# Two attention blocks with heads in halves of TensorE's rows and columns, rotation by a lane shuffle, compression in column halves

## What is computed

```python
def apply_rope(x, cos, sin):                       # on each head of 64
    x1, x2 = jnp.split(x, 2, axis=-1)
    return jnp.concatenate([x1 * c - x2 * s, x2 * c + x1 * s], axis=-1)

# layer 0, nsa_mixer: 16 query heads in 4 groups, three kinds of keys (kc, ks, kw) and values
q, kc, vc, ks, vs, kw, vw, gt = jnp.split(h @ w_in, splits, axis=-1)
def compress(t, pe, w1, w2):                       # 15 blocks of 32 tokens, every 16
    blk = (t[:, :, cidx] + pe).reshape(b, g, n_cmp, CMP_LEN * hd)
    return jax.nn.gelu(blk @ w1) @ w2
s_cmp = einsum('bgrqd,bgcd->bgrqc', q, kc) * scale # and its softmax p_cmp
o_slc = ...  # keys of chosen blocks of 64; with 256 tokens all 4 blocks are chosen: causal softmax
o_win = ...  # window of 512 over 256 tokens: causal softmax too
o = gates[0] * o_cmp + gates[1] * o_slc + gates[2] * o_win

# layer 1, swa_mixer: 16 query heads, 2 key heads, window 128, a sink for each head
p = exp(s - m); p = p / (sum(p) + exp(sink - m))
```

## Time and profile before

| | us |
|---|---|
| median of 3 runs | 1258.78 (1254.45 to 1262.51) |
| the profiled execution, whole | 1250.05 |
| its span | 1248.3 |
| PE busy in it | 1184.7 (95%) |
| DVE, ACT, POOL busy | 754.8, 564.7, 453.4 |

### The profile page before, as it was taken

The page is one execution under the profiler, slowest core; times in us unless marked ns, Lnnn a source line. Parts: engine busy times, 40 slices in busy tenths (PEclk is TensorE's granted clock), DMA queues, the critical chain, the costliest instruction groups (busy, mean ns, idle before and its releaser), DMA issues.

```text
span 1248.3 us, 23831 instructions
## 1 busy us (share of the span) xinstructions
PE 1184.7 (95%) x9314; PEld 1123.8 (90%) x9314; DVE 754.8 (60%) x1076; ACT 564.7 (45%) x789; POOL 453.4 (36%) x427
## 2 busy tenths in 40 slices
PE   7898999999999888999999999998989898999998
PEld 7896779999999865999999998997988897999998
DVE  5834664767645657676765565447664757767643
ACT  4232444545444344455454436645344544545432
POOL 5622331366620443166660211113430403666500
PEclk9997999999999989999999999999999999999999
DMA  8551102667655440466665464233432452767552
GB/s 261 174 181 34 35 1 66 203 173 196 174 182 176 146 136 1 125 179 180 190 180 180 154 193 133 76 102 102 135 102 69 135 167 72 196 174 194 176 185 85
DMA packets 226409, 175.50 MB, mean 141 GB/s; under 512 B 8720, under 2 KB 207632, under 8 KB 226208
## 3 DMA queue, kind: packets, MB, share of 16 engines
q1 hardware_dynamic: 220896, 168.89, 45.3%
q10 hardware_dynamic: 5408, 5.55, 1.4%
q0 software_dynamic: 32, 0.03, 0.0%
HBM read 173.40 MB, written 1.05 MB: 140 GB/s over the span
## 4 chain that ended last, share of the span: by engine, by line
PE 82%; DVE 8%; ACT 3%; issue 3%; POOL 3%; DMA 0%; DVEq 0%; SPq 0%; ACTq 0%; POOLq 0%
PE bank L587 22%; PE bank L593 22%; PE bank L588 22%; PE bank L862 2%; DVE w_l L1581 2%; PE bank L621 2%; ACT w_h L1204 2%; PE bank L726 1%; PE bank L1064 1%; PE bank L830 1%; PE bank L627 1%; POOL work L2346 1%; DVE work L1697 1%; PE bank L870 1%; PE bank L714 1%
## 5 line engine op out<-in xcount | busy, mean ns | idle before, releaser
L587 PE MATMUL bank<-xh,w_h 128*128 128x256 f32 (+2 forms) x1792 | 450.4, 288 | 8.4 <-ACT w_h L1256 7.0
L588 PE MATMUL bank<-xl,w_h 128*128 128x256 f32 (+2 forms) x1792 | 442.8, 284 | 0.0
L587 PEld LDWEIGHTS bank<-xh,w_h 128*128 128x128 f32 x1792 | 339.3, 189 | 11.0 <-ACT w_h L1256 7.0
L588 PEld LDWEIGHTS bank<-xl,w_h 128*128 128x128 f32 x1792 | 340.2, 190 | 0.9
L1581 DVE TENSOR_TENSOR w_l<-raw,w_h 128x2048 fp32r<-128x2048 f32 x94 | 210.3, 2237 | 160.8 <-ACT w_h L1204 160.5
L1204 ACT ACTIVATE w_h<-raw 128x2048 fp32r<-128x2048 f32 x94 | 171.4, 1823 | 229.4 <-PE bank L593 215.7
L593 PE MATMUL bank<-xh,w_l 128*128 128x256 f32 (+2 forms) x1792 | 251.4, 283 | 2.9 <-DVE w_l L1581 2.9
L593 PEld LDWEIGHTS bank<-xh,w_l 128*128 128x128 f32 x1792 | 230.5, 189 | 3.3 <-DVE w_l L1581 3.1
L2268 POOL TENSOR_TENSOR work<-work 128x256 f32<-128x256 f32 x66 | 163.0, 2470 | 139.8 <-ACT work L1351 139.8
L1865 DVE TENSOR_TENSOR w_l<-raw,w_h 128x2048 fp32r<-128x2048 f32 x66 | 151.3, 2293 | 14.0 <-ACT w_h L1347 14.0
L587 PE MATMUL bank<-hid_h,w_h 128*128 128x256 f32 (+1 forms) x592 | 147.0, 283 | 2.5 <-issue 1.8
(11 more groups left out here) (299 smaller groups left out, 1578.0 us busy)
## 6 DMA issues: line engine op xcount, KB each, us to landing
raw<-in_ffn_w_gu SPq DMA_DIRECT2D x88, 512.0 KB, 4.9
raw<-in_w_in SPq DMA_DIRECT2D x26, 1024.0 KB, 5.3
raw<-in_ffn_w_down SPq DMA_DIRECT2D x40, 512.0 KB, 4.5
raw<-in_w_ffn_up SPq DMA_DIRECT2D x22, 512.0 KB, 4.0
raw<-in_w_ffn_gate SPq DMA_DIRECT2D x22, 512.0 KB, 5.2
raw<-in_w_ffn_down SPq DMA_DIRECT2D x20, 512.0 KB, 4.6
raw<-in_nsa_w_in SPq DMA_DIRECT2D x9, 1024.0 KB, 5.5
raw<-in_swa_w_qkv SPq DMA_DIRECT2D x5, 1024.0 KB, 5.3
```

Source lines behind the costliest of these rows:

```text
L587: mm(dst, parts[0][:, k, cols], high, start=first, stop=False)
L588: mm(dst, parts[0][:, k, cols], low, start=False, stop=False)
```

## The change

- **Rotation.** Within each head the features are stored in an order in which the partner of a feature stands 16 lanes away inside the same 32 (the weights are permuted on the host, and the sine carries the sign). `permute` is gone from PE; DVE makes the partner by a `stream_shuffle` into `xr` and then multiplies by the sine.
- **Order of layer 0.** Chunks kc, vc, the eight of the queries, gates, then the keys and values. The gathering into blocks moves from DVE (16 instructions) to ACT (32 copies, before `high(4)`), without the position term, which enters as a 61st column. All loads of w1 are issued by SP, two behind slab 2 and two behind slab 4. `compress` runs twice, after chunks 7 and 11, with the blocks (61 columns) as weights and w1 (256 columns) streaming, keys into PSUM rows 0 to 60 and values into 64 to 124, one after the other in turn; then a copy, two transposes, four gelus. The scores of the compressed keys, their softmax and the first scores of pair 0 run between the last chunks; `keep_busy` before the attention is gone.
- **Attention of layer 0.** Keys keep both heads' halves in one tile without zeros; score matmuls contract over 64 rows, alternating between rows 0 to 63 (head 0, one PSUM bank) and 64 to 127 (head 1, another bank). Value products alternate between the column halves. Second and third unit get their scores together. One of three copies out of PSUM goes to ACT; the splits of slabs 11 and 12 are cut into pieces of 512 columns, one in each round. Four buffers instead of three.
- **Attention of layer 1.** One unit for each pair (both heads, both halves of the queries), 8 in all; scores of pairs 0 and 1 already run behind chunks 6 and 8 of the projections.
- Two remaining fillers are 11 and 19 matmuls of 384 columns instead of 8 and 14 of 512.

```diff
-        NSA = [(8, 1), (9, 1), (10, 0), (11, 0), ("k", 0), ("k", 2), (12, 0), (13, 0), ("k", 4), ("k", 6), (14, 0), (15, 0),
-               (16, 0)] + [(i, 1) for i in range(8)]
+        NSA = [(8, 1), (9, 1), (10, 0), (11, 0)] + [(i, 1) for i in range(8)] + [(16, 0), ("k", 0), ("k", 2), ("k", 4), ("k", 6),
+               (12, 0), (13, 0), (14, 0), (15, 0)]
...
-                mm(bank[4 + k % 2][:, 0:T1], E("rot"), xs[:, k % 2, :], start=True, stop=True).then_inc(perm_done, 1)
...
+                line.put(V.stream_shuffle(xr[:, k % 2, :], xs[:, k % 4, :], [j ^ 16 for j in range(32)]))
+                line.settle()
...
+                line.put(V.tensor_tensor(tsin[:, k % 2, :], xr[:, k % 2, :], E("sin"), ALU.mult), sin_done)
...
                 for p in range(8 * half, 8 * half + 8):
-                    for hc in range(2):
+                    for kv in range(2):
-                        last = mm(bank[7 - kv][:, 60 * hc:60 * hc + 60], w1[:, p % 8, 128 * hc:128 * hc + 128],
-                                  blkT[:, kv, p, :], start=p == 0 and hc == 0, stop=p == 15, skip_group_check=True)
+                        last = mm(bank[7][64 * kv:64 * kv + 61, 0:256], blkT[:, kv, p, :], cmp_w[half][:, kv, p % 8, :],
+                                  start=p == 0, stop=p == 15, skip_group_check=True)
...
+                for b in range(2):
+                    for a in range(2):
+                        last = mm(bank[4 + a][:, 128 * b:128 * b + 128], q_half(ci, a, 0), k_half(4 * b + ci // 2, a, 128),
+                                  start=False, stop=True, skip_group_check=True)
...
+                for b in range(2):
+                    for kb in range(2):
+                        for a in range(2):
+                            at = 256 * b + 128 * kb
+                            last = value_piece(O, a, 1, S_pt[:, (p + a) % 4, at:at + 128], b, kb, g)
...
+            for i in range(1, 8 + 2):
+                if i <= 8:
+                    part_turn(3 * i - 3)
+                if i < 8:
+                    first_scores(i)
+                if i >= 2:
+                    second_values(i - 2)
+                if i <= 8:
+                    part_turn(3 * i - 2)
+                if i < 8:
+                    second_scores(i)
+                if i <= 8:
+                    first_values(i - 1)
+                    part_turn(3 * i - 1)
...
+                for i in range(2, 8 + 2):
+                    pair_turn(i - 2)
+                    if i < 8:
+                        pair_scores(i)
+                    pair_values(i - 2)
```

More of the change, by code:

```diff
@@ L610, in chunk @@
                 line["n"] += 1
-            def keep_busy(b, n):
-                for _ in range(n):
-                    mm(bank[b][:, 0:512], ident_b[:, :], mask_b[:, 0:256].unsqueeze(1).broadcast_to([128, 2, 256]), start=True,
-                       stop=True, skip_group_check=True)
             def turn(ins, signal):
@@ new lines, in _ @@
+                if n == 18:
+                    cmp_turn()
+                    pe.wait_ge(cmp_kv_taken, 6)
+                    pe.wait_ge(vt_taken, 1)
+                    first_scores(0)
+                if n >= 19:
+                    w = n - 19
+                    if w:
+                        second_scores(0)
+                    pe.wait_ge(proj_taken, 19 + 2 * w)
+                    turn([(bank[2 + w][:, 256 * kb + 128 * j:256 * kb + 128 * j + 128],
+                              big1[:, 12 + 2 * w + j, 128 * kb:128 * kb + 128]) for kb in range(2) for j in range(2)], vt_done)
@@ new lines, in _ @@
+            high(2)
+            high(3)
+            act.wait_ge(meta_ss, 1)
+            line.put(fn(meta_rstd[:, :], bank[6][:, 0:META], ACT.Sqrt, bias=eps_col[:, 0:1]), meta_root)
+            act.wait_ge(proj_taken, 4)
+            blocks(1)
+            act.wait_ge(roped, 2)
+            blocks(0)
+            high(4)
+            high(5)
+            high(6)
+            high(7)
+            act.wait_ge(cmp_hid, 2)
+            act.wait_ge(prepared, 4)
+            for kv in range(2):
+                at = slice(64 * kv, 64 * kv + 61)
+                line.put(fn(hid_sb[at, :], bank[7][at, 0:256], ACT.Copy), cmp_raw)
@@ new lines, in _ @@
+            high(8)
+            act.wait_ge(vt_done, 1)
+            line.put(fn(egate.rearrange("p a b -> p (a b)"), bank[5][:, 0:96], ACT.Exp, scale=-1.0), vt_taken)
+            act.wait_ge(cmp_hidt, 1)
+            hid = bank[6][:, 0:256].rearrange("p (h k c) -> p h k c", h=2, k=2)
+            line.put(fn(pe_b, hid[:, :, :, 60], ACT.Copy))
+            line.settle()
+            for kv in range(2):
+                for hc in range(2):
+                    line.put(fn(hidT[:, kv, hc, :], hid[:, hc, kv, 0:60], ACT.Gelu_apprx_tanh, bias=pe_b[:, hc, kv:kv + 1]), cmp_act)
@@ L1333, in _ @@
-            attention(NSA_UNITS, 0, True, 0)
+                line.put(fn(vc_rep[32 * r:32 * r + NCMP, :], bank[4][0:NCMP, 0:256], ACT.Copy), cmp_kv_taken)
+            fn(scrap, eps_col[:, 0:1], ACT.Exp)
+            high(10)
+            act.wait_ge(cmp_centered, 1)
+            line.put(fn(c_e, c_s, ACT.Exp, scale=SCALE), cmp_exp)
+            for qb in range(2):
+                act.wait_ge(cmp_turned, qb + 1)
+                line.put(fn(c_pt[:, qb, :, :].rearrange("p a b -> p (a b)"), bank[6 + qb][:, :], ACT.Copy), cmp_pt)
@@ L1447, in _ @@
                              vt_taken)
-            attention(SWA_UNITS, V_SWA, False, 8)
+                if n == 8:
+                    pair_exp(0)
+            pair_exp(1)
+            for i in range(2, 8 + 3):
+                if i >= 3:
+                    attention_high(i - 3, False)
+                if i < 10:
+                    ci = i - 2
+                    act.wait_ge(at_turned, V_SWA + 2 * ci + 2)
+                    if ci >= 2:
+                        act.wait_ge(at_pv, 16 + ci - 1)
+                    line.put(fn(S_pt[:, 2 * (ci % 2) + 1, 0:384], bank[3][:, 0:384], ACT.Copy), at_pt_act)
+                if i < 8:
+                    pair_exp(i)
             squares(3, T1, xT, taken(N_SWA_O), lambda c: high(M_SWA + 7 + c // 2) if c % 2 else None)
@@ L2232, in ropes @@
                     else:
+                        if table is NSA:
+                            pool.wait_ge(cmp_hid, 2)
                         for g in range(2):
```

776 lines of the change are left out of this document (414 added, 362 removed).

## The result

| | before | changed |
|---|---|---|
| median, first measurement | 1256.62 us (1253.60 to 1262.51, 4 runs) | 1222.49 us (1212.78 to 1227.75, 4 runs) |
| the same, measured again | 1252.57 us (1244.88 to 1262.57, 11 runs) | 1223.74 us (1215.69 to 1227.43, 6 runs) |
| profiled execution, whole | 1250.05 | 1217.23 |
| its span | 1248.3 | 1215.4 |

The changed kernel is faster: its time over that of the kernel before, the ratio, is 0.9732 with a 95% interval of 0.9684 to 0.9780, and 0.9764 (0.9720 to 0.9809) when measured again. The prediction was 1207 us with a range of 1190 to 1228. In the profiled executions 32.8 us are saved; the forecast was 51.7.

A forecast was written before the change was run, and what follows sets the result against it. PE was taken to bound layer 0's attention, PE and the chain together layer 1. Savings of 41.4 us (layer 0) and 10.3 (layer 1), 51.7 of 1250.05, gave 1198.4 profiled, scaled to a median of 1207 us, range 1190 to 1228.

The forecast's parts named there:

- PE's list in the projections of layer 0: Layer 0 from 17.8 us: chunks 54.0, compression 6.9, moved-in work 10.2 and small items, in all 74.7 us of PE work.
- Its waits: PE's expected waits in the projections of layer 0: sum 11.8 us, less 1 that overlaps, 10.8.
- 74.7 + 10.8: Layer 0 projections: PE's work plus waits, added to the 17.8 us start, put the attention rounds' start at 103.3 us.
- Compression: Layer 0: 64 passes of 0.217 us, 13.9 serially, 6.9 with column halves overlapping; ACT copies together 8 us.
- A round: Layer 0's attention: PE work 6.3 us, no gain taken for first scores; 6.6 us taken per round.
- the chain: Layer 0's attention, round to round: transposes, first scores, maximum, ACT, evacuation and wait, gates, POOL, hand-overs; given as 6.6 us.
- Layer 1: Attention start about 9.5 us behind the last chunk, 3.85 us a pair, end at 485.4 us instead of 495.7: 10.3 less.
- rival 3: DVE and ACT become the bound: a round of 8.2 us, projections lose 10 more, 1228 us in all; 14%.
- 1: Array halves don't overlap when changing at every matmul: round 9.3 us on PE, compression 13.9, 1237 us in all; 5%.
- 2: Each change of half drains the array, 0.14 us a change, 38 us on top of non-overlapping halves: 1275 us; 3%.
- 4: Gaps in the new rounds keep PE's clock low: round 11.0 us, layer 1 pair 5.3, 1251 us in all; 4%.
- 5: More gain than forecast: no waits in the projections and rounds of 5.9 us, 1190 us in all; 4%.

The follow-up runs named there:

- the kernel with all orders: Changed kernel with layer 1's start reordered, layer 0's waits removed, maximum ahead of factor, and three more edits of order; 1201.58 us, ratio 0.9594.

## Why the prediction was right, and where it was off

The median of 1222.5 us lies inside the range and 15.5 above the forecast. In the profiled execution 18.9 us of the forecast are missing: 9.5 in layer 0, 6.8 in layer 1, 2.5 behind.

- **PE's list in the projections of layer 0: right, a little high.** The sum was 74.7 us. In the kernel with all orders, where the clock is 1.00, the stage takes 74.2 with its last 1.4 us of waits, and PE's work is 72.8.
- **Its waits: five of six there, their price on the clock missing.** Forecast 1.3 us for `low(2)`, 2 ahead of the compression, 1.7 the gates, 1 the gelus, 3.8 the softmax, 2 the values; measured 1.06 (in two parts), 2.73, 1.81, none, 4.62, 1.94. The softmax's own terms (1.9 + 2.3 + 4.8 - 5.7) give 3.3, not 3.8. The total of idle time was 12.2 us against 10.8. But PE's busy time was 78.5 instead of the 72.8 that the same list takes at full clock: behind waits part of the work ran at the lower clock (granted 0.92 in the stage). "74.7 + 10.8" added waits to work at full clock. Rounds started at 108.8 instead of 103.3.
- **How much that price is, differs by execution.** Behind the wait of 4.6 to 4.7 us the transposes took 1.97 us in all nine profiles that have it, against 1.03 without it. Behind the 2.7 us wait the first compression took 5.29 us (granted 0.68 in it) in the first profile, and 3.60 in the second, at full clock:

```profile
40.20 3.67 PE L735 MATMUL psum<-big,work 128*61 128x256 f32 x32 [2.76 <-ACT work L1316]
```

  The second compression took 3.61 in the first profile. In the second one and in four of the edited kernels with the same projections the rounds start at 105.8 to 105.9 us and PE is busy for some 75.6. So of the 5.5 us by which the rounds were late in the first profile, 3.0 were that execution's, and the stage's waits cost about 2.8 us of clock in the others.
- **Compression: right.** 2 x 3.6 us at full clock against 6.9 forecast; the copies on ACT took 9.05 us against 8. They were expected to start near 30 us, when slab 3 has landed; ACT waited 4.4 us for that slab and they started at 31.1.
- **A round: right in what bounds it not, off in the chain.** PE's work was forecast at 6.3 and is 6.2. The forecast took no gain for the first scores; there is one, 0.64 us instead of 1.09. The chain was given as 6.6 us through transposes, scores and POOL, but its terms as listed (0.53, 1.24, 0.9, 1.4, 0.4, 0.6, 0.4, 1.04, 0.5) add up to 7.0. The real one is a ring through DVE and ACT of 7.09; that 7.0 lies near it is chance, since the links are others. The step that failed is the list of links: it lacked the order on DVE (the maximum behind the last factor) and DVE's being held by POOL, 2 x 0.34 us. The whole attention took 55.5 us against 51.5, of which the six rounds make 2.9 (6 x 0.49); the rest lies in the first round, which ran partly at the lower clock (granted 0.64 from 108.8 to 112.0), and in the tail.
- **Layer 1: pairs right, the start wrong.** The step that failed is the list of what stands in DVE's and POOL's order there. A pair 3.75 us against 3.85, PE's work 3.1 against 3.0, the 3.6 us wait in front of the third chunk gone. The gap at the start was 14.9 instead of 9.5, by the links named above; the projections were 1.0 longer.
- **The number.** That 1222.5 us lies inside the range is owed to its width: it reaches 21 us above the forecast to take in most of rival 3. The saving is 32.8 us of 51.7 in the profiled executions; PE's work and the pairs of layer 1 were right, and what was missing were waits, their price on the clock and the links of the round.
- **Rivals.** 1 and 2 are out: halves overlap, and the run in blocks of row halves shows no saving from fewer changes. The drain at each change of tiling mode that the Trainium skill names (TensorEngine Tiling (Array Packing), Key Properties) may be in the 0.2 us that a group costs over its passes: 1.07 - 4 x 0.217 for the second scores alternating, 1.93 - 8 x 0.217 in one half. No run separates it from other costs of a group. By Gotcha 1 of the same page of the Trainium skill two row tiles cannot access one PSUM bank at once. One after the other the two compressed values would have taken 2 x 0.57 = 1.14 us, by the price in the kernel before; they took 0.58 in one bank, and that they were both being written at the same instant is not shown. 3 came true in kind: its reason, that DVE works in order for other engines, is what the ring shows, and its size, 8.2 us a round, is not (7.09). 4 came true in small pieces outside the steady rounds. 5 did not; the kernel with all orders, at 6.55 us a round and nearly without waits in the projections, comes near it in layer 0.

## What to carry to other kernels

When TensorE's work in a loop shrinks below the other engines', write down the ring that closes from one round to the next, with each in-order neighbour as a link; the load of an engine, here 6.1 of 7.09 us, tells less than its order. Moving one instruction past its neighbour was worth 0.54 us a round, taking 0.6 us of work away nothing. A wait on TensorE is to be priced with the work behind it, which may run at the lower clock for a while: here waits of 12.2 us went with 2.8 to 5.8 us more of busy time. And an improvement of a few us is to be read in the stage: the whole varied by 15 us from run to run of one kernel, and the stages that no edit touched by 11 between profiles.

## What the runs showed of the hardware that was not expected

- Two halves of the array overlap without alternating, if the block in one half is short: 4 passes fully (1.07 us either way for row halves, 0.59 for column halves), 6 and 8 in part (1.05 against 0.80, 1.48 against 1.02), 16 hardly (6.31 against 3.6).
- Row halves overlap even with 128 columns to stream, where a pass costs as much as one of 60 columns (0.112 and 0.109 us): eight passes 0.64 us instead of 1.09.
- DVE and POOL hold one another up, and by kinds of instruction rather than by size. A `TENSOR_SCALAR` of 2 or 4 elements a lane took 0.51 instead of 0.17 us and ended with POOL's instruction; a sine product, which reads two tiles of SBUF, took 0.82 to 0.94 instead of 0.43. DVE's reductions and copies from PSUM beside POOL were not held, nor was a shuffle that reads and writes SBUF (0.44 us from 410.54, inside a POOL instruction from 410.36 to 411.09 that took its usual 0.73, and 0.43 to 0.44 alone). In the other direction, POOL's sum took 2.73 us instead of 0.72 while a `low` ran. By the Trainium skill (SBUF — State Buffer, SBUF: two separate sides) the two compete for one pair of ports, which whoever starts first holds for a whole instruction; on DVE's side it names instructions with two inputs in SBUF and those in a certain fast mode. The trace agrees, with these numbers; whether the small product ran in that mode, no run shows. DVE's and then POOL's timeline of the changed kernel:

```profile
47.54 2.28 DVE L1677 TENSOR_TENSOR w_l<-raw,w_h 128x2048 fp32r<-128x2048 f32 x1
```

```profile
47.70 2.73 POOL L2381 TENSOR_TENSOR big<-work 128x256 f32<-128x256 f32 x1 [0.36 <-DVE work L1744]
```

- A `stream_shuffle` of 256 columns takes 0.44 us beside a forecast of 0.4.
